# A hybrid decoder step on one core: dilated keys and values loaded in another order, the first half's values multiplied one step sooner, window loads and key gathers begun at other points

## The reference, cut to what matters

```
DILATED_PATTERNS = ((128, 1), (512, 4), (2048, 16))
def _dilated_sample(q, k_cat, v_cat, buf_len, bias_a):
    for window, dil in DILATED_PATTERNS:
        idx = buf_len + jnp.arange(t)[:, None] - j[None, :] * dil
        kg, vg = k_cat[:, idx], v_cat[:, idx]
        logits = einsum('bthd,btnhd->bthn', q, kg) * ATT_SCALE + bias
        probs, lse = _masked_softmax(logits, valid)
        outs.append(einsum('bthn,btnhd->bthd', probs, vg)); lses.append(lse)
    return _merge_by_denominator(outs, lses)
```

## Time and profile before

| | |
|---|---|
| median of three runs | 2094.52 us |
| the profiled execution | 2091.84 us, of it span 2090.0 us |
| TensorE busy in the span | 2030.1 us (97%) |
| compressed_and_dilated on TensorE | 502.9 to 613.8 us |
| sample_selected on TensorE | 613.8 to 794.0 us |

### The profile page before, as it was taken

The page is one execution under the profiler, slowest core; times in us unless marked ns, Lnnn a source line. Parts: engine busy times, 40 slices in busy tenths (PEclk is TensorE's granted clock), DMA queues, the critical chain, the costliest instruction groups (busy, mean ns, idle before and its releaser), DMA issues. The chain is left out here.

```text
span 2090.0 us, 31740 instructions
## 1 busy us (share of the span) xinstructions
PE 2030.1 (97%) x12334; PEld 1325.8 (63%) x12334; DVE 1113.5 (53%) x2524; ACT 520.4 (25%) x1140; POOL 578.9 (28%) x753
## 2 busy tenths in 40 slices
PE   7999999999989989999999999999999999999998
PEld 3445466666556666766776458888888888634443
DVE  4035455421535546777775467777776766511452
ACT  4111010101333435776675031111111111000001
POOL 2444234202025740112232441322222222304110
PEclk9999999999999999999999999999999999999999
DMA  9376677663699994233343126666665422601111
GB/s 255 118 237 258 263 289 277 242 214 124 229 365 387 419 409 162 70 92 92 93 143 112 29 81 221 221 211 213 218 205 202 142 81 62 242 4 30 43 40 41
DMA packets 154296, 373.04 MB, mean 178 GB/s; under 512 B 34885, under 2 KB 92989, under 8 KB 136093
## 3 DMA queue, kind: packets, MB, share of 16 engines
q1 hardware_dynamic: 126420, 149.63, 22.8%
q0 software_dynamic: 25472, 149.45, 18.4%
q10 hardware_dynamic: 2256, 71.94, 9.8%
HBM read 343.68 MB, written 98.60 MB: 212 GB/s over the span
## 5 line engine op out<-in xcount | busy, mean ns | idle before, releaser
L2981 PE MATMUL ff_ps<-ff_hx,whole_aw 128*128 128x264 f32 x2464 | 550.5, 386 | 0.8 <-DVE ff_hx L3377 0.8
L2981 PEld LDWEIGHTS ff_ps<-ff_hx,whole_aw 128*128 128x128 f32 x2464 | 467.1, 190 | 80.6 <-issue 1.2
L837 DVE STREAM_TRANSPOSE whole_space<-whole_space 128x512 f32<-128x512 f32 x256 | 155.3, 674 | 153.6 <-PE late_bank L637 153.6
L601 PE MATMUL late_bank<-in_w,in_xT 128*128 128x512 f32 (+1 forms) x512 | 201.6, 547 | 0.0
L1224 DVE CUSTOM_DVE_ANT_0 pa_L<-late_bank,whole_space 128x512 f32<-128x512 f32 (+3 forms) x288 | 141.0, 532 | 43.4 <-PE late_bank L1070 41.8
L601 PEld LDWEIGHTS late_bank<-in_w,in_xT 128*128 128x128 f32 x512 | 95.1, 191 | 95.0 <-issue 88.4
L1196 ACT ACTIVATE pa_L<-pa_L,pa_nm 128x640 f32<-128x640 f32 (+3 forms) x192 | 142.0, 741 | 47.0 <-DVE pa_nm L1236 46.7
L3007 PE MATMUL ff_ps<-ff_hx,whole_space 128*128 128x512 f32 x336 | 148.0, 593 | 0.0
L717 ACT ACTIVATE in_yout<-late_bank 128x128 f32<-128x128 f32 (+5 forms) x88 | 40.9, 479 | 380.7 <-PE late_bank L601 200.2
L3461 DVE SCALAR_TENSOR_TENSOR whole_space<-whole_space,ff_kept 128x1024 f32<-128x1024 f32 x88 | 123.1, 1399 | 3.1
L637 PE MATMUL late_bank<-whole_space 128*64 128x256 f32 (+1 forms) x1152 | 121.6, 364 | 0.0
(11 more groups left out here) (441 smaller groups left out, 2670.0 us busy)
## 6 DMA issues: line engine op xcount, KB each, us to landing
out_new_a_k_s<-in_cache_a_k ACTq DMA_DIRECT2D x8, 4088.0 KB
out_new_a_v_s<-in_cache_a_v ACTq DMA_DIRECT2D x8, 4088.0 KB
whole_aw<-in_w_up SPq DMA_DIRECT2D x44, 512.0 KB, 7.4
in_w<-in_w_in SPq DMA_DIRECT2D x5, 2048.0 KB, 13.0
whole_space<-in_cache_a_k SPq DMA_DIRECT2D x8, 1024.0 KB
whole_space<-in_cache_a_v SPq DMA_DIRECT2D x8, 1024.0 KB
ff_hx<-in_w_down SPq DMA_DIRECT2D x14, 512.0 KB, 4.2
whole_space<-in_x_prompt SPq DMA_DIRECT2D x12, 512.0 KB, 10.2
```

Source lines behind the costliest of these rows:

```text
L601: mm = pe.matmul(ps[0:n, b, 0:width], xT[:, k, t * P:t * P + n], w[:, at % WBUF, k, 0:width], start=(k == 0), stop=(k == KC - 1))
L837: last = dve.transpose(put[:, dh, :, k * HD:k * HD + HD].rearrange("p t (g b) -> p t g b", g=2), got[:, :, :, dh, :])
L2981: mm = pe.matmul(ps[:, bank_of(x, j, g), 0:H2], aw[:, j % 2, at, k, :], hx[:, bt, k, g * H2:g * H2 + H2], start=(k == 0), stop=(k == KH - 1))
```

## The change

- probs(0) moves from the end of step 5 to the end of step 4, on TensorE, ScalarE and VectorE (turning). values(0) moves from the start of step 6 to step 5, between keys(5, 0) and scores(4, 1). The second half stays where it was.
- d_pv counts items instead of halves, so each value item gives its slot free by itself.
- SP loads in the order 5, 7, 8, 9, 10, 6, 11, 12 to 15, all of them ahead of the wait for choice and pen's store. win_v is loaded ahead of win_k, once K6 is transposed, and no longer behind the stores of scr_mixc.
- GpSimd's first two gathers wait for values(0) alone, and the next two for V4's product alone.

```diff
+        turning = (4, 9)
@@ use, on_act and the same condition in probs on PE, ACT and DVE
-                if s == 5 + 4 * g:
+                if s == turning[g]:
@@ free_after
-            return (d_tr, use["keys", g * 4 + j, NTL - 1] + 1) if kv == 0 else (d_pv, g + 1)
+            return (d_tr, use["keys", g * 4 + j, NTL - 1] + 1) if kv == 0 else (d_pv, 4 * g + j + 1)
@@ gpsimd
-            pool.wait_ge(d_tr, use["keys", NB - 1, NTL - 1] + 1)
-            pool.wait_ge(d_pv, 1)
+            pool.wait_ge(d_pv, 4)
             for c in range(2):
                 pre.gather_keys(pool, 0, c)
+            pool.wait_ge(d_tr, use["keys", NB - 1, NTL - 1] + 1)
             ahead.retire()
             pool.sem_inc(ops.s_retired, 1)
-            pool.wait_ge(d_pv, 2)
+            pool.wait_ge(d_pv, 5)
@@ sync
-            for i in range(5, 12):
+            for i in (5, 7, 8, 9, 10, 6, 11, 12, 13, 14, 15):
...
                 load(i)
             sp.wait_ge(s_v, 17)
...
-            for i in range(12, 16):
-                load(i)
...
+            sp.wait_ge(d_tr, use["keys", NB - 2, NTL - 1] + 1)
+            pre.load_window(sp, "cache_win_v", pre.value, pre.s_wv)
             sp.wait_ge(d_tr, use["keys", NB - 1, NTL - 1] + 1)
             pre.load_window(sp, "cache_win_k", pre.key, pre.s_wk)
...
-            pre.load_window(sp, "cache_win_v", pre.value, pre.s_wv)
@@ tensor, values(g)
-                mm.then_inc(d_pv, 1)
+                    mm.then_inc(d_pv, 1)
@@ tensor, the steps
+                if s == 10:
+                    values(1)
                 for g in range(2):
-                    if s == 6 + 4 * g:
-                        values(g)
...
                 if s < NB:
                     keys(s, 0)
+                if s == 5:
+                    values(0)
                 if 1 <= s <= NB:
                     scores(s - 1, 1)
@@ scalar and vector: the waits on d_pv in items
-                            act.wait_ge(d_pv, g)
+                            act.wait_ge(d_pv, 4 * g)
```

10 lines of the change are left out of this document (5 added, 5 removed).

## The result

| | before | changed |
|---|---|---|
| median | 2092.47 us (2087.34 to 2097.07, 6 runs) | 2102.2 us (2098.97 to 2105.76, 6 runs) |
| ratio, 95% interval | | 1.0042, 1.0024 to 1.006 |
| profiled execution | 2091.84 us, span 2090.0 us | 2098.97 us, span 2097.1 us |

The account below looks back on a forecast made before the run. TensorE, busy 97% of the span, was taken to bound the kernel up to 658 us, the full DMA from there. 2.8 + 3.4 + 3.2 - 4.3 = +5.1 us gave 2099.6 us in the median's terms, range 2089 to 2108 us.

Parts of the forecast that it names:

- A: keys(5, 0): TensorE waits for VectorE, which now does prompt_maxima and block_probs after the PT copies; cost 2.8 us.
- B: keys(6, 0): values(0) no longer covers VectorE's prompt_weights and choice, so TensorE waits; cost 3.4 us.
- The clock: After each of the two new TensorE waits, matmuls run at a lower clock: 1.6 us each, 3.2 us together.
- Loads one by one: Value loads V0 to V7 all land before values(0) and values(1) need them, V4 to V7 going out later; worth 0.
- From there the full DMA sets the pace: From 658 us, where a gather waits for sequence 0's product, the DMA bounds; only TensorE's time before that was summed.
- Term C: Earlier gathers remove TensorE's waits for gathered keys at 637.92 and 645.55 us, with their clock loss; gain 4.3 us.
- Rival 3: Start of sample_selected: SP's queue issues win_k late, TensorE waits 13 us; sum +18.1 us, 2112.6 us; chance 0.13.
- Rival 1: TensorE's idle gap in values(1) goes too, with its clock loss, 4.5 us; sum +0.6 us, 2095.1 us; chance 0.17.
- Rival 2: The DMA bounds sample_selected; four gathers moved into free time save 10 us, A and B vanish; 2084.5 us; chance 0.10.
- Rival 4: Term C gives nothing, since TensorE's waits follow GpSimd's gather rate; sum +9.4 us, 2103.9 us; chance 0.15.

Follow-up runs that it names:

- e4: Changed kernel with prompt_maxima and block_probs ahead of the PT copies, block_sums ahead of values(0), prompt_weights and choice ahead of keys(5, 1)'s copies: 2099.5 us, 1.0028.
- e3: Changed kernel with VectorE's prompt_maxima and block_probs back ahead of the copies into PT: 2097.5 us, 1.0021.
- e6: Changed kernel with GpSimd's first two gathers back behind K7's last transposes: 2103.8 us, 1.0072.
- e9: Changed kernel with win_k issued ahead of win_v in SP's program: 2100.3 us, 1.0035.
- e8: As e1, with pen stored ahead of V4 to V7: 2098.2 us, 1.004.
- e1: Changed kernel with probs(0) and values(0) back in their old steps 5 and 6; loads and gathers as changed: 2086.9 us, 0.998.
- e2: Changed kernel with the old order of SP and GpSimd; probs(0) and values(0) stay moved: 2103.8 us, 1.005.
- e12: Kernel before with one more 2.1 MB copy behind win_v, for which nothing waits: 2098.0 us, 1.0032.
- e11: As e8, with the new keys and win_k issued before SP waits for pen, and win_v behind it: 2095.7 us, 1.0013.

## Why the prediction was right or wrong

**The number is right, the account behind it is not.** 2099.6 us was forecast and 2102.2 us measured.

- **Terms A and B.** The waits were sized well: 2.33 us for 2.8, 3.17 us for 3.4. As terms of a sum along TensorE they fail: covering both moves TensorE 9.1 us and the product by nothing (e4). B doesn't count, since it stands behind V4's issue; A counts by the delay that it gives V4 (e3).
- **The clock.** In the changed kernel it cost 1.56 us behind A and 1.5 us behind B (3.00 + 1.52 us, where 2.00 us and 1.06 us are usual for such rows), for the 1.6 us of each. Behind A that is luck in part: in e6 and e9 the same wait had no slow matmuls behind it, and the kernel before has a slow stretch at this place without the wait, 0.57 from 553 to 557 us, in which 16 transposes took 3.41 us. The prediction counted its own and not that one.
- **"Loads one by one", V4 "also 0".** This is the step that failed. The prediction asked only whether V4 to V7 come in time for values(1). They do. But V4's issue is the start of some 90 us in which the DMA is nearly always full, up to the first values(0) of sample_selected, and where little else changes the end follows the start: 8.9 us later at V4 gave 8.2 us at the product (e8 against e1), 12.1 us gave 11.6 us (e2 against before). V4 went out at 70.7 us instead of 67.4 us, and that is 3.3 us of the loss; the other 6.9 us are the length, 94.2 us instead of 87.3 us, which comes with the new order of SP and GpSimd (e2, with the old order, has 86.8 us). The sum had no term for either.
- **"From there the full DMA sets the pace", from 658 us.** The DMA was already full at 580 us, at 1.05, and the prediction read it there as a rate only. e12 shows that in this stretch transfers are paid for. The place that the prediction named is right as an end, since 136.4 us follow from there in both; the pace is set ahead of it too.
- **Term C.** No wait for gathered keys stands ahead of the first values(0), as forecast. But the 4.3 us did not come back: 3.47 us for win_k with its slow window transposes (5.64 us for 32 where e1 takes 4.02), and 1.56 us for a late VectorE copy (below) took their place.
- **Rival 3.** Its mechanism came, at 3.47 us: win_k was issued at 599.24 us and was all in at 621.08 us, 21.8 us for which the prediction's best case had 11 us, since it left the 2.1 MB of scr_mixc stores behind it and the two gathers at 606.82 us out of the sum. The prediction had named such a wait as a sign of being wrong, and so it was, of the account. Its price didn't come: e9 takes the wait away and gains nothing measurable. While SP stood for pen behind V4 to V7 the DMA idled 3.0 us at 594 us.
- **Rival 1** didn't come: the gap recurs. **Rival 2**, that gathers carry time across, has something in it: in e6 the stretch from V4 is 2.5 us longer without the first pair's early start, but the rest of the change takes more. **Rival 4** (2103.9 us) was nearer to the median than the forecast, by chance of the sum.

That the number fell within 2.6 us is luck in good part. 5.1 us were forecast, and 7.1 us came in the profiled execution and 9.7 us in the medians. The terms behind the 5.1 us are 9.4 us on TensorE, of which only what delays V4 reaches the product, and 4.3 us of gain that didn't come; the start of V4 and the length behind it, which made the loss, stood at 0. Two slips in its sums change nothing: term B takes off 6.0 us where its text has 6.1, and rival 3 starts from 590.9 us where 575 + 15.1 is 590.1.

What stays open: e1's median is 5.7 us below that of before, and its profiled execution only 2.2 us below, with the product 1.2 us later and the first key transposes 3.1 us sooner. Counted from cd_qp its product is 1.3 us sooner than before's (108.6 and 110.0 us); the rest of why e1 is faster isn't shown by the places in the table. Why the length grows by 6.9 us is bookkeeping of idle DMA time only: filling one hole opened another (e9). The runs of one kernel spread over up to 18 us (e11: 2088.95 to 2106.64), so that a place read from one profile is good to a few microseconds at best.

## What to carry to other kernels

Where a stretch is full on the DMA, take its length apart as start, busy time and idle time: the first load's issue, bytes that no order changes, and the holes in which a queue stands for a semaphore or a slot. Here an edit of the compute order was worth what it did to the start and the holes, and waits covered on TensorE behind the start turned up again at a later transfer. A test that costs one run is to add a copy that nobody waits for: if the time grows by its bytes, the DMA is the bound there, whatever the busy shares of the engines say. Put it where no transfer that is needed stands behind it on its queue. And before two profiles are compared, compare them at a place that the edit can't have moved.

## What the runs showed of the hardware

**A VectorE copy held by GpSimd.** VectorE and GpSimd of the changed kernel, in time:

```profile
634.89 2.72 DVE L2451 COPY sb_work<-sb_Ln 128x4 f32<-128x4 f32 x1
```
```profile
635.06 2.51 POOL L2143 TENSOR_TENSOR sb_work<-sel_BS,sample_kcs 128x512 f32<-128x512 f32 x2
```

The copy of 128x4 took 0.16 us in the kernel before. Here it ends at 637.61 us, with GpSimd's second operation (637.57 us), and TensorE waited 1.56 us for what stands behind it. It took 2.71 to 2.72 us in e3 to e6 too, each time beside two operations of GpSimd. The Trainium skill (SBUF — State Buffer, SBUF: two separate sides) says that the two engines share a pair of ports as an exclusive lock, where one that starts first has it for a whole instruction and the other blocks fully. The trace agrees on the block, with 2.56 us added. It shows more than the sentence says: the copy's record starts 0.17 us ahead of GpSimd's first operation, and it waited for both.

**A gap of TensorE inside a run of matmuls, with a full DMA.** values(0) is 256 matmuls with no wait inside. In e8 it took 8.14 us in a stretch with the DMA at 0.04; in e1, with V4 in flight, it broke for 2.15 us (e8, then e1):

```profile
563.05 8.14 PE L1596 MATMUL late_bank<-whole_space,cd_PT 128*32 128x128 f32 x256
```
```profile
570.39 4.54 PE L1594 MATMUL late_bank<-whole_space,cd_PT 128*32 128x128 f32 x82 [2.15 <-issue]
```
```profile
566.00:570.00 4.00, 2.25 (x73) 1.58 (x62) 1.79 (x11) 0.00 (x0) 0.00 (x0) 1.00 1.03 331
```

values(1), always under a full DMA, breaks in its third item in every kernel, by 0.37 us (e11) to 3.46 us (e2), in 13 of the 14 ahead of the last 117 matmuls. A full DMA alone isn't enough: in the kernel before, sample_selected's 128 matmuls at 673.34 us took 3.68 us without a break, at a DMA share of 1.02. What the sequencer waits for isn't named in the trace, and wasn't tried. A candidate is the program's own code: the profile's queue "instruction" moved one packet in the 2 us in which the break begins in the kernel before (604 to 606 us), the changed kernel (608 to 610 us) and e1 (568 to 570 us). It moved none from 602 to 606 us in e4, whose break is 0.41 us, and one from 674 to 676 us in the kernel before, where nothing broke. That is not a proof.
